# Cutting a GpSimd weight-splitting instruction into four quarters, in a two-layer hybrid model on one core

## What is computed

```python
def hybrid_layer(x, ...):                       # first layer
    z = rmsnorm(x, g_mix) @ w_in                # 7 parts of 1024 columns
    # per head of 4: convolution, gates, a linear recurrence over time, a second convolution
    x = x + merged @ w_out
    g, u = jnp.split(rmsnorm(x, g_ffn) @ w_gate_up, 2, axis=-1)
    x = x + (jax.nn.silu(g) * u) @ w_down
    return x + jax.nn.sigmoid(rmsnorm(x, g_ple) @ w_ple_gate) * (p_i @ w_ple)

def hybrid_layer_2(x, ...):                     # second layer
    proj = rmsnorm_2(x, norm1_gain) @ w_in      # queries, keys, values of two attentions
    o_a, o_b = nsa_mixer(...), mla_mixer(...)
    h = x + mixed @ w_out
    return h + peer_ffn(rmsnorm_2(h, norm2_gain), peer_w_q, peer_sub_keys, peer_u, peer_v)
```

## Time and profile before

| what | us |
|---|---|
| median of 3 runs | 2495.98 (2493.74 to 2496.31) |
| profiled execution, whole | 2498.66 |
| its span, first to last instruction | 2496.9 |
| PE busy in the span | 2432.8 |
| DVE busy | 1699.2 |
| POOL busy | 1100.9 |
| ACT busy | 858.3 |
| POOL in L2217 (x167 into `spl`) | 193.2 |
| POOL in L2219 (x167 into `spl`) | 432.6 |

### The profile page before, as it was taken

One profiled execution on the slowest core, in us unless ns is written; L12 is line 12 of the kernel. 1 busy time (PEld: TensorE's weight loads), 2 busy tenths in 40 slices (PEclk: granted clock), 3 DMA queues, 4 the chain that ended last, 5 costly groups with the idle time before them and its releaser, 6 DMA issues.

```text
span 2496.9 us, 36678 instructions
## 1 busy us (share of the span) xinstructions
PE 2432.8 (97%) x13021; PEld 2138.8 (86%) x13021; DVE 1699.2 (68%) x2879; ACT 858.3 (34%) x1497; POOL 1100.9 (44%) x671
## 2 busy tenths in 40 slices
PE   6999999999999999899899999999999999999999
PEld 5877887888887887555689999999999999999999
DVE  6867675462433553776753699888886787877877
ACT  3333232100113324676324333344443333333332
POOL 4666666665664551000363788841112333232331
PEclk9999999999999999999999999999999999999999
DMA  3333323433432223000132799999999999999995
GB/s 127 102 102 102 100 86 128 136 111 111 137 104 94 79 78 119 1 1 1 59 93 87 232 308 312 306 334 341 345 343 398 385 351 336 343 345 345 338 343 195
DMA packets 181335, 490.43 MB, mean 196 GB/s; under 512 B 14848, under 2 KB 80512, under 8 KB 181248
## 3 DMA queue, kind: packets, MB, share of 16 engines
q1 hardware_dynamic: 144384, 355.12, 42.5%
q0 software_dynamic: 36864, 134.23, 14.3%
HBM read 436.86 MB, written 52.43 MB: 196 GB/s over the span
## 4 chain that ended last, share of the span: by engine, by line
PE 89%; issue 4%; POOL 3%; DVE 3%; ACT 1%; DMA 0%; DVEq 0%; SPq 0%; ACTq 0%; POOLq 0%
PE ps L593 38%; PE ps L1101 38%; POOL spl L2282 2%; PE ps L1029 2%; PE ps L1122 2%; PE ps L685 1%; PE ps L1006 1%; PE ps L992 1%; DVE st L1962 1%; POOL rare L2292 1%; PE ps L784 1%; PE ps L951 1%; PE ps L746 1%; PE ps L988 1%; PE ps L897 0%
## 5 line engine op out<-in xcount | busy, mean ns | idle before, releaser
L593 PE MATMUL ps<-hh,spl 128*128 128x512 f32 x1840 | 575.8, 393 | 10.6 <-DVE hl L2000 6.4
L1101 PE MATMUL ps<-wsp,spl 128*128 128x384 f32 x3072 | 539.7, 336 | 0.9 <-DVE spl L2117 0.8
L1101 PE MATMUL ps<-hh,spl 128*128 128x384 f32 x2048 | 535.5, 337 | 2.9 <-POOL spl L2282 2.7
L1101 PEld LDWEIGHTS ps<-wsp,spl 128*128 128x128 f32 x3072 | 530.4, 188 | 8.2 <-DVE wsp L2174 5.7
L1469 ACT ACTIVATE spl<-ring 128x1024 fp32r<-128x1024 f32 x256 | 271.7, 1061 | 694.0 <-PE ps L1101 692.0
L2217 POOL CAST spl<-ring 128x1024 fp32r<-128x1024 f32 (+1 forms) x167 | 193.2, 1157 | 649.1 <-PE ps L593 559.2
L2219 POOL TENSOR_TENSOR spl<-ring,spl 128x1024 fp32r<-128x1024 f32 (+1 forms) x167 | 432.6, 2590 | 13.4
L593 PEld LDWEIGHTS ps<-hh,spl 128*128 128x128 f32 x1840 | 347.9, 189 | 88.2 <-DVE hl L2000 7.3
L1101 PEld LDWEIGHTS ps<-hh,spl 128*128 128x128 f32 x2048 | 370.9, 188 | 6.3 <-issue 5.3
L593 PE MATMUL ps<-hl,spl 128*128 128x512 f32 x920 | 360.1, 391 | 0.0
L1101 PE MATMUL ps<-hl,spl 128*128 128x384 f32 x1024 | 342.5, 334 | 0.0
(11 more groups left out here) (381 smaller groups left out, 3232.8 us busy)
## 6 DMA issues: line engine op xcount, KB each, us to landing
ring<-stream_in SPq DMA_DIRECT2D x134, 512.0 KB, 3.5
ring<-u_in SPq DMA_DIRECT2D x128, 512.0 KB, 5.6
ring<-v_in SPq DMA_DIRECT2D x128, 512.0 KB, 6.0
ring<-stream_in SPq DMA_DIRECT2D x60, 704.0 KB, 4.1
gelu<-gst SPq DMA_DIRECT2D x128, 192.0 KB, 5.9
dense<-stage SPq DMA_DIRECT2D x12, 2048.0 KB, 12.6
gl<-gelu SPq DMA_DIRECT2D x32, 768.0 KB, 6.9
gw<-dense SPq DMA_DIRECT2D x32, 768.0 KB, 9.3
```

The costliest lines, as they stand in the source:

```text
L593: m = pe.matmul(ps[:, bank, :], w[:, part, k0 + k * n:k0 + k * n + P], rhs(k), start=first and k == 0 and part == 0 and rhs is high, stop= ...
L1101: m = pe.matmul(ps[:, bank, 0:TD], w[:, part, k0 + k * P:k0 + (k + 1) * P], rhs(k), start=first and k == 0 and part == 0 and rhs is high, ...
```

## The change

The subtraction that makes the low part of a unit is written as four subtractions of a quarter of the columns each. The four follow each other with no wait between them, and the last one alone reports `wt_low`.

```diff
                 w = spl[:, j % 2, :, :] if w is None else w
                 pool.tensor_copy(w[:, 0, 0:n], ring[:, j, 0:n]).then_inc(wt_high, 1)
                 pool.wait_ge(wt_high, count)
-                pool.tensor_tensor(w[:, 1, 0:n], ring[:, j, 0:n], w[:, 0, 0:n].bitcast(F32), ALU.subtract).then_inc(wt_low, 1)
+                for k in range(4):
+                    cols = slice(k * n // 4, (k + 1) * n // 4)
+                    m = pool.tensor_tensor(w[:, 1, cols], ring[:, j, cols], w[:, 0, cols].bitcast(F32), ALU.subtract)
+                m.then_inc(wt_low, 1)
```

## The result

| what | before, us | after, us |
|---|---|---|
| median of 5 runs each | 2495.60 (2493.74 to 2496.31) | 2509.42 (2508.78 to 2512.47) |
| ratio | 1 | 1.0058, 95% interval 1.0043 to 1.0073 |
| span of the profiled execution | 2496.9 | 2507.6 |
| DVE busy | 1699.2 | 1573.7 |
| POOL busy | 1100.9 | 1230.4 |

The change makes the kernel 13.8 us (0.6%) slower. The forecast was 2508.5. DVE is busy for 125 us less and POOL for 130 more, and the first is worth next to nothing where PE is the bound. Of all executions behind these and the later numbers one, of the kernel with unit 67 whole, ran far slower than the rest (4523.48 us, granted clock 0.81); it is left out of every comparison.

What follows compares the result with a forecast made beforehand. PE was taken to bound the four heads, with POOL's work hidden. Losses of 11.6, 1.6 and 0.8 less 1.5 regained make 12.5 us, so 2508.5 for the median, range 2497 to 2520.

Steps and rivals of the forecast that it cites:

- The bound: In the four heads, 23 to 355 us, PE is always busy and POOL's work hidden: nothing to win, only lose.
- Room per unit: POOL's slack behind PE: 1.25 us at unit 11, 0.52 at unit 12; a stall is about 0.31 less the room.
- The quarter's price: POOL's quarter subtraction: 0.65 us each in plain succession, 0.25 more per unit; 0.60 each when alternating with DVE.
- the dear quarters: Rival: DVE and POOL alternate, but waiting doesn't hide start-up; a quarter takes about 0.75 us, total 2518.7; chance 0.13.
- the other estimate: From the Trainium skill's 4497 ns for 2048 columns: 0.3 us fixed per POOL instruction, 0.9 more per unit; not adopted.
- Turns: DVE gets one instruction between POOL's quarters, 0.55 us each, a scan 1.08; forecast case, 2501 to 2514, chance 0.60.
- The rival of no turns: POOL keeps the ports between quarters and loses only its overhead: 2496.0 to 2498.9 us, likeliest 2496.5; chance 0.18.
- The four heads: First stage: stalls 1.39 at unit 11, 1.13 at 12, 0.36 at 15, 11.6 us in four heads; first convolutions 1.6 more.
- Unit 65: Behind the heads, counted among the other units: about one DVE instruction at most, which fits into the room; loss 0.
- Unit 67: Unit PE already waits for: 0.25 us for the quarters and 0.55 for L1609 getting in, 0.8 in all.
- L1879: Ahead of the attention, PE's 1.9 us wait shrinks because L1947 slips in between quarters: 1.5 us back.
- The sum: Whole program: 11.6 + 1.6 + 0.8 - 1.5 = 12.5 us slower, 2508.5 us for the median.

Runs made afterwards that it cites:

- lengthened: Kernel before, low part still one instruction but 1216 columns instead of 1024, two memsets added at the start: 2498.72 us, ratio 1.0014.
- narrow kernel: Changed kernel with DVE's in-place instructions of the four heads cut from 512 columns to 8: 2500.25 us, ratio 1.0014 to the kernel before.

## Why the prediction came true, step by step

**The bound.** Right. PE was the bound, POOL's work was hidden, and only a loss was to be had: kernels with quarters from unit 68 on alone show the most that can be gained, 0.06% by the ratio, and it can't be told from nothing.

**Room per unit.** Right. A stall of 0.31 less the room, from rooms of 1.25 and 0.52, gave the places and the sizes.

**The quarter's price.** In turns, 0.60 was right within 0.02: unit 11's CAST ends at 77.26 + 1.27 = 78.53 and its last quarter at 83.58, 5.05 for my 5.13; less 2.73 of guests (three at 0.55, a scan at 1.08) that is 0.58 a quarter. Alone I had 0.65 each and 0.25 more per unit. Measured it is 2.82 for the four against 2.40, 0.42 more, between my 0.25 and the 0.75 of the dear quarters, and less than half of the 0.9 that the other estimate in the prediction gave. It cost nothing in the heads, where a wait covers it, but unit 67 shows it: its low part took 2.69 and takes 3.55,

```profile
390.18 3.55 POOL L2221 TENSOR_TENSOR spl<-ring,spl 128x256 fp32r<-128x256 f32 x4
```

0.86 more with one guest more than before (L1609, between the third and the fourth quarter), for which the sum had 0.8.

**Turns.** Right. The reading that carried it was one row, a DVE instruction that ended between two POOL instructions that had no pause between them. The guests of units 11 and 12 and their order are those of the sum, one by one. The rival of no turns is out: DVE's L1660 takes 1.11, where it took 2.78.

The Trainium skill (SBUF — State Buffer, Who interferes with whom) says that the holder of the shared ports keeps them for a whole instruction. The lengthened and the cut kernel agree: the unit of exclusion was the instruction, 3.15 us when it was long and some 0.6 when it was cut.

**The four heads.** 13.2 forecast (11.6 + 1.6), 13.2 measured in both traces of after; the single steps are within 0.15 of the sum's. Units 13 and 14 lose nothing, as I said, but only because 11 and 12 had already let DVE's chain through; leaving those whole showed that.

**Unit 65: the step that failed.** The prediction said: "The other units meet at most about one such DVE instruction, and 0.25 + 0.55 fit into their room." I had looked for short rooms in the heads and assumed that behind them the pattern holds. There it doesn't: PE takes only the first 18 of 24 matmuls of units 64, 65 and 66 before it returns for the rest, so it wants unit 65 a quarter of a unit sooner, and four DVE instructions (L1662, L1663, two L1669) meet it, not one. The low part takes 4.47, PE waits 1.79, and 1.6 us are missed.

**Unit 67.** PE's wait grew by 0.87 for 0.8. The lowered clock behind the longer wait, 1.4 to 1.6 in the two traces of after, wasn't in the sum.

**L1879.** 1.43 for 1.5 in the first trace, 1.1 in the second. In before one instruction of the chain is held for a whole instruction of POOL; with quarters L1947 starts before the next quarter, and L1948 alone is held, for the rest of that quarter:

```profile
1008.62 0.26 DVE L1947 TENSOR_TENSOR rt<-kcn,rope 128x62 f32<-128x62 f32 x1
1008.91 0.73 DVE L1948 TENSOR_TENSOR kcn<-rt 128x62 f32<-128x62 f32 x1
```


**The sum.** What the trace shows of the change itself is 13.2 + 1.6 + 0.9 - 1.4 = 14.3, and about 1.5 of clock at unit 67, 15.8 in all; I forecast 12.5. Unit 65 and that clock are what I missed. The medians differ by 13.8, and the interval of the ratio is worth 10.7 to 18.2 us, so the medians can't tell 12.5 from 15.8; only the traces can. In the first pair of traces a clock that was lowered less at other places hid 5 us of the loss; in the pair taken again, with spans of 2509.0 and 2493.9, it hid far less. How much of that is in the medians isn't shown. The turns were right, and that the forecast came within 1 us of the time was luck.

## What to carry to other kernels

Cutting a long GpSimd instruction doesn't only add its start-up: it hands the shared ports to VectorE at every cut. Do it where VectorE's chain is what is waited for, and leave it whole where GpSimd's result is; before the attention here four pieces won 1.1 to 1.4 us and two won nothing, in the heads four lost 13. Read the room of every unit, those behind a loop's end too, and don't expect to mend it by undoing the worst ones: the other engine's chain arrives later and takes its turns from the next.

## What the runs showed of the hardware that I had not expected

- Turns are strict and need no pause: with eight pieces at unit 11 one instruction of DVE went ahead of each of them, eight in all, and four pieces stretched from 2.82 to 4.97 us (0.55 a turn, 1.08 a scan), though POOL's next piece starts in the profile some 0.04 us before the one ahead ends.
- With nobody beside, POOL's subtraction took 2.81 us for 1216 columns, 2.40 for 1024, 0.74 for 256 and 0.46 for 128: about 2.1 ns a column and some 0.2 us for each instruction (an estimate from these four).
- A small instruction of DVE waits as long as a large one, but costs POOL next to nothing (the quarters beside it took 0.74 as alone). In the narrow kernel two of 8 columns, the second of which falls between CAST and the first quarter:

```profile
82.54 0.82 DVE L1659 TENSOR_TENSOR hs<-hs,z_ry 128x8 f32<-128x8 f32 x1
83.39 0.17 DVE L1660 TENSOR_TENSOR hs<-hs,z_gr 128x8 f32<-128x8 f32 x1
```

- After PE had waited for 2.85 us or more at unit 67, its granted clock fell to half, 1.2 GHz, in all nine traces, and after 2.72 us in one of five. Each fall cost 1.4 to 2.9 us.
- Executions of the kernel before differ by up to 6 us (2493.06 to 2499.14 in 27 runs), and where traces of one kernel differ, beside their starts (1.9 us between the earliest and the latest of fourteen traces), it is in steps of about 1.6 us where PE's clock was lowered in one and not in the other. The 1.1 to 1.4 us won at L1879 can be seen in a trace and not in a median.
